# Two feature blocks side by side at stage starts, and matmuls with fixed operands in TensorE's waits

## The reference, cut to what matters

```python
for i in range(DEPTH):                        # 2
    a = rmsnorm(h, norm_mix_pre[i])
    m = forgetting_attention(a, ...) if i % 2 == 0 else gated_deltanet(a, ...)
    h = h + rmsnorm(m, norm_mix_post[i])
    f = conv_ffn(rmsnorm(h, norm_ffn_pre[i]), ffn_w_up[i], ffn_conv[i], ffn_w_down[i])
    h = h + rmsnorm(f, norm_ffn_post[i])
def conv_ffn(h, w_up, conv_w, w_down):
    u = causal_dwconv(h @ w_up, conv_w)
    gate, up = jnp.split(u, [FFN_DIM], axis=-1)
    return (jax.nn.gelu(gate, approximate=True) * up) @ w_down
# second part: h = x @ w_in ("latents", mla_mixer), then moba_mixer; after each
x = layer_norm(ALPHA * x + y, ln_g[layer], ln_b[layer])
```

## Time and profile before

| | |
|---|---|
| median of 3 runs | 1336.22 us (1335.25 to 1338.72) |
| the profiled execution | 1336.22 us |
| its span, first to last instruction | 1334.4 us |
| PE busy | 1202.0 us (90%) |
| DVE busy | 919.2 us (69%) |
| ACT busy | 747.5 us (56%) |
| mean granted TensorE clock | 0.948 of full |
| DMA | 160.24 MB, mean 120 GB/s |

### The profile page before, as it was taken

How to read it: one execution, slowest core, us unless ns; L and a number is a source line. 1 busy time by engine, 2 the same in 40 slices (tenths; PEclk the granted TensorE clock), 3 DMA queues, 4 the chain that set the end, 5 groups by cost and what they waited for, 6 DMA issues and landing times.

```text
span 1334.4 us, 26401 instructions
## 1 busy us (share of the span) xinstructions
PE 1202.0 (90%) x9237; PEld 1128.9 (85%) x9237; DVE 919.2 (69%) x1710; ACT 747.5 (56%) x1531; POOL 76.1 (6%) x76
## 2 busy tenths in 40 slices
PE   5599996999999688886998979999978999799996
PEld 5588886999999578875997869999978999699995
DVE  4888875777753678778543567876466787677874
ACT  6377755566644487867214346665444665455543
POOL 0300000112100000000200001121000000000000
PEclk8799998999999889988899789999989999999998
DMA  6233323355565233333000216555643444334430
GB/s 241 88 114 106 126 80 126 97 179 169 165 174 141 85 110 106 110 97 120 12 1 1 80 50 187 185 179 175 176 139 107 127 135 148 126 111 135 145 114 32
DMA packets 49965, 160.24 MB, mean 120 GB/s; under 512 B 5488, under 2 KB 8432, under 8 KB 49776
## 3 DMA queue, kind: packets, MB, share of 16 engines
q1 hardware_dynamic: 49904, 159.44, 37.8%
HBM read 158.37 MB, written 1.05 MB: 119 GB/s over the span
## 4 chain that ended last, share of the span: by engine, by line
PE 75%; issue 15%; DVE 6%; ACT 2%; POOL 1%; DMA 0%; SPq 0%; ACTq 0%; DVEq 0%; POOLq 0%
PE bank L354 20%; PE bank L356 19%; PE bank L355 19%; PE bank L412 3%; PE bank L1381 2%; PE bank L1389 2%; PE bank L856 2%; PE bank L836 1%; DVE rstd L429 1%; PE bank L821 1%; ACT w_hi L335 1%; DVE w_lo L340 1%; PE bank L1397 1%; PE bank L818 1%; DVE q_n L1085 1%
## 5 line engine op out<-in xcount | busy, mean ns | idle before, releaser
L354 PE MATMUL bank<-x_hi,w_hi 128*128 128x272 f32 (+2 forms) x1624 | 489.4, 301 | 68.7 <-DVE x_lo L457 28.6
L340 DVE TENSOR_TENSOR w_lo<-raw,w_hi 128x1024 fp32r<-128x1024 f32 (+5 forms) x332 | 370.1, 1122 | 210.0 <-ACT w_hi L335 209.5
L356 PE MATMUL bank<-x_hi,w_lo 128*128 128x272 f32 (+2 forms) x1624 | 473.5, 292 | 0.0
L355 PE MATMUL bank<-x_lo,w_hi 128*128 128x272 f32 (+2 forms) x1624 | 473.0, 291 | 0.0
L354 PEld LDWEIGHTS bank<-x_hi,w_hi 128*128 128x128 f32 x1624 | 315.6, 194 | 86.1 <-issue 46.4
L335 ACT ACTIVATE w_hi<-raw 128x1024 fp32r<-128x1024 f32 (+5 forms) x332 | 314.4, 956 | 95.2 <-PE bank L356 90.0
L355 PEld LDWEIGHTS bank<-x_lo,w_hi 128*128 128x128 f32 x1624 | 317.4, 195 | 0.2
L356 PEld LDWEIGHTS bank<-x_hi,w_lo 128*128 128x128 f32 x1624 | 316.6, 195 | 0.0
L354 PE MATMUL bank<-hid_hi,w_hi 128*128 128x272 f32 (+1 forms) x352 | 102.7, 292 | 0.0
L356 PE MATMUL bank<-hid_hi,w_lo 128*128 128x272 f32 (+1 forms) x352 | 100.7, 286 | 0.0
L355 PE MATMUL bank<-hid_lo,w_hi 128*128 128x272 f32 (+1 forms) x352 | 100.2, 285 | 0.0
(11 more groups left out here) (278 smaller groups left out, 1911.7 us busy)
## 6 DMA issues: line engine op xcount, KB each, us to landing
raw<-w_up SPq DMA_DIRECT2D x88, 512.0 KB, 3.9
raw<-w_attn SPq DMA_DIRECT2D x32, 512.0 KB, 4.7
raw<-w_dn SPq DMA_DIRECT2D x32, 512.0 KB, 3.9
raw<-w_moba SPq DMA_DIRECT2D x32, 512.0 KB, 4.0
raw<-w_down SPq DMA_DIRECT2D x32, 384.0 KB, 3.2
raw<-w_down SPq DMA_DIRECT2D x32, 320.0 KB, 3.2
raw<-w_mla SPq DMA_DIRECT2D x16, 384.0 KB, 3.3
raw<-w_attn_out SPq DMA_DIRECT2D x8, 512.0 KB, 4.4
```

Of the source, the lines that this page charges most:

```text
L340: nc.vector.tensor_tensor(w_lo[:, q, 0:wd], raw[:, q, 0:wd], w_hi[:, q, 0:wd].bitcast(F32), ALU.subtract).then_inc(lo_done, 1)
L354: nc.tensor.matmul(dst, hi, src[0][:, k, c0:c1], start=first, stop=False)
L355: nc.tensor.matmul(dst, hi, src[1][:, k, c0:c1], start=False, stop=False)
L356: return nc.tensor.matmul(dst, lo, src[0][:, k, c0:c1], start=False, stop=last)
```

## The change

`keep_clock(count)` issues `count` matmuls of `ones_r` with 256 fixed columns into bank 6, which nothing reads. They wait for nothing. The three constant matrices are laid in one buffer, so that 256 columns stand side by side. Nine calls stand in TensorE's program between stages, 268 matmuls in all. Beside that, the first two blocks of both feed-forward layers, of the latents and of attention 2 (queries and keys) are made by `two_products`: for each input tile k, the three matmuls of the first block and then the three of the second.

```diff
-        ones_r = ctx.enter_context(nc.sbuf_tensor("ones_r", [P, P], F32R))
-        sum_gc_r = ctx.enter_context(nc.sbuf_tensor("sum_gc_r", [P, P], F32R))
-        sum_beta_r = ctx.enter_context(nc.sbuf_tensor("sum_beta_r", [P, C], F32R))
+        fixed_r = ctx.enter_context(nc.sbuf_tensor("fixed_r", [P, 2 * P + C], F32R))
+        ones_r, sum_gc_r, sum_beta_r = fixed_r[:, 0:P], fixed_r[:, P:2 * P], fixed_r[:, 2 * P:2 * P + C]
...
+        def keep_clock(count):
+            for _ in range(count):
+                nc.tensor.matmul(bank[6][:, 0:2 * P], ones_r, fixed_r[:, 0:2 * P], start=True, stop=True)
...
             def step(p):
-                queries()
-                if not first:
-                    pe_scores(pe, f, p - 1)
-                keys()
+                if first and f == 2:
+                    pe.wait_ge(q_ready, 16)
+                    pe.wait_ge(k_ready, 16)
+                    two_products(pe, "w_moba", (bank[0][:, 0:SEQ], bank[1][:, 0:SEQ]), (META, T), X_BASE["ln1"])
+                else:
+                    queries()
+                    if not first:
+                        pe_scores(pe, f, p - 1)
+                    keys()
                 values()
...
+        def two_products(pe, name, dsts, cols, x_base):
+            for k in range(KT):
+                pe.wait_ge(x_ready, x_base + k + 1)
+                for q, dst in enumerate(dsts):
+                    if k == 0:
+                        weights_here(pe, name, 0, q)
+                    mm = product(dst, q, k * P, x_op, k, cols, k == 0, k == KT - 1)
+                    if k == KT - 1:
+                        mm.then_inc(chunk_used, 1)
...
-            unit(0)
+            if f:
+                pe.wait_ge(conv_done, FT * f)
+            two_products(pe, name, (bank[0][:, c0:c1], bank[1][:, c0:c1]), cols, X_BASE[f"pre{2 * f + 1}"])
+            unit(0, (1,))
...
         def latent_pe(pe):
             c0, c1 = META, T
-            for j in range(KT):
-                if j >= 2:
-                    pe.wait_ge(sq_ready, sq0["lat_q"] + j - 1)
+            two_products(pe, "w_latent", (bank[0][:, c0:c1], bank[1][:, c0:c1]), (c0, c1), X_BASE["post3"])
+            lat_sum(pe, 0)
+            for j in range(2, KT):
+                pe.wait_ge(sq_ready, sq0["lat_q"] + j - 1)
...
             tail_pe(pe, 0, "w_attn_out", "post0", FULL, False)
+            keep_clock(36)
             sums_pe(pe, "pre1", KT, FULL)
+            keep_clock(28)
             ffn_pe(pe, 0)
+            keep_clock(32)
             sums_pe(pe, "pre2", KT, FULL)
+            keep_clock(28)
             pe.wait_ge(tables_in, 16)
             dn_pe(pe)
+            keep_clock(36)
             sums_pe(pe, "pre3", KT, TAIL)
+            keep_clock(28)
             ffn_pe(pe, 1)
+            keep_clock(38)
             latent_pe(pe)
             attention_pe(pe, 1)
             tail_pe(pe, 1, "w_mla_out", None, LAST, True)
+            keep_clock(14)
             sums_pe(pe, "var1", KT, LAST)
+            keep_clock(28)
             attention_pe(pe, 2)
```

More of the change, by code:

```diff
@@ L811, in pe_scores @@
                 for hh in range(2):
-                    nc.tensor.matmul(bank[5 - hh][:, 0:SC], ones_r[:], rows_a[:, p * 2 + hh, :], start=True, stop=False)
+                    nc.tensor.matmul(bank[5 - hh][:, 0:SC], ones_r, rows_a[:, p * 2 + hh, :], start=True, stop=False)
             for b, ((q0, q1), (s0, s1)) in enumerate(part):
@@ L863, in aw @@
                     pe_.wait_ge(lat_ready, k + 1)
-                elif f == 2:
-                    pe_.wait_ge(x_ready, X_BASE["ln1"] + k + 1)
             def step(p):
@@ L1202, in ffn_pe, with unit @@
             name = f"w_up{f}"
-            def unit(u):
-                for r in range(2):
+            def unit(u, sides=(0, 1)):
+                for r in sides:
                     g = u * 2 + (r + FT * f)
@@ L1212, in unit @@
                         for k in range(KT):
-                            if isinstance(u, int) and u == 0 and q == 0:
-                                pe.wait_ge(x_ready, X_BASE[f"pre{2 * f + 1}"] + k + 1)
                             mm = product(bank[q][:, c0:c1], q, k * P, x_op, k, cols, k == 0, k == KT - 1)
                         mm.then_inc(chunk_used, 1)
-            unit(0)
+            if f:
+                pe.wait_ge(conv_done, FT * f)
+            two_products(pe, name, (bank[0][:, c0:c1], bank[1][:, c0:c1]), cols, X_BASE[f"pre{2 * f + 1}"])
+            unit(0, (1,))
             with pe.Fori(1, FT // 2) as u:
@@ L1322, in prepare @@
                 wait(pe, dn["qk"], d)
-                nc.tensor.matmul(bank[4][:, 0:TP], sum_gc_r[:], rows_d[:, d, :], start=True, stop=True).then_inc(dn["row"], 1)
+                nc.tensor.matmul(bank[4][:, 0:TP], sum_gc_r, rows_d[:, d, :], start=True, stop=True).then_inc(dn["row"], 1)
                 for c in range(NC):
@@ L1339, in prepare_keys @@
                 pe.wait_ge(dn["dec_t"], 3 * d + 3)
-                nc.tensor.matmul(bank[4][0:C, 0:TP], sum_beta_r[:], rows_d[:, d, :], start=True, stop=True).then_inc(dn["beta"], 1)
+                nc.tensor.matmul(bank[4][0:C, 0:TP], sum_beta_r, rows_d[:, d, :], start=True, stop=True).then_inc(dn["beta"], 1)
             def step(d):
@@ L1814, in latent_pe @@
             c0, c1 = META, T
-            for j in range(KT):
-                if j >= 2:
-                    pe.wait_ge(sq_ready, sq0["lat_q"] + j - 1)
+            two_products(pe, "w_latent", (bank[0][:, c0:c1], bank[1][:, c0:c1]), (c0, c1), X_BASE["post3"])
+            lat_sum(pe, 0)
+            for j in range(2, KT):
+                pe.wait_ge(sq_ready, sq0["lat_q"] + j - 1)
                 weights_here(pe, "w_latent", j // 4, j % 4)
                 for k in range(KT):
-                    if j == 0:
-                        pe.wait_ge(x_ready, X_BASE["post3"] + k + 1)
                     mm = product(bank[j % 2][:, c0:c1], j % 4, k * P, x_op, k, (c0, c1), k == 0, k == KT - 1)
                 mm.then_inc(chunk_used, 1)
-                if j:
-                    lat_sum(pe, j - 1)
+                lat_sum(pe, j - 1)
             lat_sum(pe, KT - 1)
@@ L1938, in constants_and_first_weight @@
                 act.wait_ge(s_in, 32)
-                nc.scalar.activation(ones_r[:], ones, ACT.Copy).then_inc(ones_ready, 1)
-                nc.scalar.activation(sum_gc_r[:], tb("sum_gc"), ACT.Copy).then_inc(ones_ready, 1)
-                nc.scalar.activation(sum_beta_r[:], tb("sum_beta"), ACT.Copy).then_inc(ones_ready, 1)
+                nc.scalar.activation(ones_r, ones, ACT.Copy).then_inc(ones_ready, 1)
+                nc.scalar.activation(sum_gc_r, tb("sum_gc"), ACT.Copy).then_inc(ones_ready, 1)
+                nc.scalar.activation(sum_beta_r, tb("sum_beta"), ACT.Copy).then_inc(ones_ready, 1)
                 prime(act, "pre0")
```

## The result

The changed kernel takes 1322.85 us (median of 4 runs, 1321.68 to 1324.42), against 1336.18 us of the kernel before (4 runs, 1335.25 to 1338.72): a ratio of 0.990, with a 95% interval of 0.988 to 0.992. The forecast was 1323.5 us. The profiled execution took 1321.68 us, its span is 1319.9 us, and the mean granted clock went from 0.948 to 0.966.

A forecast was written before the change was run, and what follows sets the result against it. TensorE was taken to set the time inside stages, DVE's chain of norm, root and inverse the idles between. Sums 2.05 plus pairs 10.7 make 12.7 us off 1336.22: 1323.5 us, range 1319.5 to 1331.

The forecast's parts named there:

- The price of a fixed matmul: In the nine idles between stages: 0.122 us each, above 0.126, so all runs fit and cost nothing.
- The third rival: At the nine idles: each fixed matmul costs 0.23 us and overruns, 20.4 us more, 1343.9 us; chance 0.06.
- The clock holds at the nine places: At the nine filled idles: with only 0.5 to 1.3 us of idle left, the clock stays up.
- The first rival: At the stage starts: the clock falls as before, gain 2 us in all, 1334.2 us; chance 0.09.
- the second: Rival at the stage starts: the clock falls at some places, half of the 10.7 us, 1328.8 us; chance 0.17.
- The sums at full clock: Three groups of eight sums ahead of stages: gains of 0.45, 0.95 and 0.65 us, sum 2.05 us.
- The pairs: First two blocks of both feed-forward layers, latents, attention 2: gains of 2.5, 2.4, 2.4, 3.4 us, together 10.7 us.
- The new wait in the latents: Ahead of the latents' first sum: TensorE waits for ACT's copy and square, 0.5 us, bounds 0 and 0.9.
- What follows has its inputs: Behind the paired blocks: later work finds its inputs ready; DeltaNet gets only its earlier start.
- Elsewhere: Places without fixed matmuls: clock falls stay and may move, taken as 0, with 4 us either way.
- The price of 0.4 us for a fall in a DeltaNet step: In DeltaNet's steps: 19.93 us without a clock fall, 20.29 with one, so 0.4 us each.
- DeltaNet steps of more than 20.3 us: In DeltaNet: steps this long were named as a sign that the prediction is wrong.

The follow-up runs named there:

- e4_half_more: The changed kernel with one and a half times each count of fixed matmuls; 1324.07 us.
- e1_blocks_only: The changed kernel without any fixed matmul, the pairs of blocks kept; 1334.78 us.
- e3_half: The changed kernel with half of each count of fixed matmuls; 1331.20 us.
- e2_fixed_only: The changed kernel with the fixed matmuls but the blocks one after the other, as before; 1333.35 us.
- e5_out_and_second: The changed kernel plus fixed matmuls: 20 ahead of attention 1, 22 ahead of DeltaNet's output-norm spreading, 4 behind each of its first seven steps; 1328.28 us.
- e7_all_and_steps: The changed kernel plus fixed matmuls ahead of attention 1, in DeltaNet's output, most other idles, and 13 in each DeltaNet step but the first; 1322.17 us.

## Why the prediction was right, point by point

- **The price of a fixed matmul** was taken as 0.122 us, at most 0.126; it is 0.125. All nine runs lie inside DVE's waits. The third rival (0.23 each, an overrun, 1343.9 us) is excluded by that row alone. (Its sum took three idles from like places; the trace of before has 4.71, 4.06 and 5.29 us there, 40.3 in all and not 41.2.) e4_half_more adds that an overrun would have cost far less than the rival said: 1.2 us by the medians for 134 matmuls too many.
- **The clock holds at the nine places**: right, 1.00 in all nine waits, the sums and the four pairs. That it does not hold without the fixed matmuls is shown by e1_blocks_only and e3_half; that they are not enough at the latents without the second block, by e2_fixed_only. The reason given, idles left of 0.5 to 1.3 us, is borne out only as far as these nine places go. The first rival and the second stood for kernels like e1 and e3; they gave 1334.2 and 1328.8 us, and these measured 1334.8 and 1331.2. The first agreement is luck: the pairs gained 5.2 us instead of 2, and falls at other places took much of it back.
- **The sums at full clock**: 5.71, 6.23 and 5.92 us became 5.46, 5.47 and 5.25 (the second is the stretch from 441.55 to 447.02 us). Gains 0.25, 0.76 and 0.67, together 1.68 where 2.05 was said. The term that was mis-sized is the first, and with it the second, which was built on it: the end of the last sum behind the last square was set at 0.65 us and is 1.0 (227.86 to 228.85), since the last three squares come back to back and their sums queue.
- **The pairs**: gains of 2.36, 2.33, 2.15 and 3.36 us against 2.5, 2.4, 2.4 and 3.4. All are 0.04 to 0.25 short: the pairs ran up to 0.16 us longer than worked out. (The latents' third block in before starts at 999.31, not at 999.07, behind a sum of 0.24 us; both 9.92 and 7.77 count the sum in.) For attention 2 the prediction put half of the 3.4 us on the clock; the full clock alone gave 0.76 there (e2_fixed_only) and the order alone 2.29, with a fall still in it (e1_blocks_only). Its wait ahead grew by 0.15 us, which the sum had at nothing. The order of banks cost no pause: 48 matmuls of layer 1's pair are 5.89 us of work in 5.90. The prediction had weighed against this the Trainium skill, "TensorE: Matmul & The Clock Gate", section "A second HAM failure mode: psum-queue depth-cycling"; the trace does not bear it out for this form of alternation.
- **The new wait in the latents** was put at 0.5 us. The row of the changed kernel below has 0.39 of idle behind the last matmul's end, 0.55 behind the end of its place in the queue (986.61 + 0.12 to 987.28). Right.

```profile
987.28 0.70 PE L411 MATMUL bank<-sq,tab 128*128 128x256 f32 x2 [0.39 <-ACT sq L402]
```

- **What follows has its inputs**: right. The rest of layer 0 takes 195.63 us in both kernels.
- **Elsewhere**: taken as 0 ± 4 us. From DeltaNet's first product to the sums behind its output it was 1.44 us shorter than before, from the latents' third block to the layer norm's sums 0.43 longer, and attention 0, from its first sum on, 0.44 shorter. No instruction of TensorE was changed in these stretches. The clock fell in them at other moments and for other lengths: at the start of attention 1 for 6.8 us instead of 3.4. How far such a stretch moves without any edit is seen in DeltaNet up to the end of its solve, 273.3 to 277.4 us in eight kernels. So the ± 4 us was a fair size, and 0 a choice. The price of 0.4 us for a fall in a DeltaNet step was wrong: it was read from one step without a fall, of 19.93 us, while before itself has a step of 19.64 us with a fall (521.03 to 540.67), and the later traces show 0.7 us or nothing, by where the fall lies. The sign "DeltaNet steps of more than 20.3 us" told nothing for the same reason: before has one of 20.31, the changed kernel one of 20.33.

So the terms that the prediction named come to 1.68 + 10.2 = 11.9 us of the 12.7. In the two profiled executions another 1.4 us come from the stretches elsewhere, and 1.2 from the earlier start. Being 0.65 us off by the medians is better than the terms deserve: they were 0.8 too high, and the part that was set at zero made up for it. That is luck.

Where the reasoning failed was behind the result, in e5_out_and_second to e7_all_and_steps: I carried the rule "fill what is idle" into a loop whose matmuls fill only 8 rows, and counted at full clock what ran at half.

## What to carry to other kernels

Where a stage starts behind a norm, ask two things together: does TensorE's clock come through the wait, and does the first block leave TensorE idle between its input tiles. The two blocks side by side alone were worth 1.8 us here, the fixed matmuls alone 3.2, both 13.3. Filler of full-size matmuls is nearly free in a wait that another engine sets, even when it overruns a little; halving it lost nearly two thirds of the gain. Inside a loop that another engine paces, compare a turn at the lower clock, filler included, with that pace before adding any. And compare kernels by stretches that have the same program in both: the same DeltaNet moved by 4 us with the falls of the clock inside it, more than most of the gains looked for.
